# Token transforms split by symmetry, and a short convolution taken from the in-projection's banks

## The reference, cut to what matters

```python
def fourier_mix(u):                       # over tokens (L) and over 64-wide groups of channels
    g = u.reshape(B, L, FNET_GROUPS, FNET_GROUP_W)
    return jnp.fft.fftn(g, axes=(1, 3), norm="ortho").real

def hyena_mix(u, conv_w, conv_b, ..., d_bias):
    u = short_conv(u, conv_w, conv_b)     # out[t] = b + w0*u[t-1] + w1*u[t] + w2*u[t+1]
    x0, x1, v = jnp.split(u, 3, axis=-1)
    z = x1 * v
    k = hyena_filters(L, ...)             # an MLP of positions, times a decay, divided by its absolute sum
    y = irfft(rfft(z, 2L) * rfft(k, 2L))[:, :L] + d_bias * z
    return x0 * y
```

## Time and profile before

| | |
|---|---|
| median of 3 runs | 2781.29 us |
| profiled execution, its own time | 2783.26 us |
| its span | 2781.4 us |
| TensorE busy | 2525.0 us (91%) |
| VectorE, ScalarE, GpSimd busy | 1321.5, 909.1, 580.7 us |
| in-projection of layer 0 and 1 | 903.7 to 1039.3 and 1998.2 to 2100.5 us |
| `mid` of layer 0 and 1 | 1039.3 to 1147.2 and 2100.5 to 2185.9 us |

### The profile page before, as it was taken

The page is one execution under the profiler, slowest core; times in us unless marked ns, Lnnn a source line. Parts: engine busy times, 40 slices in busy tenths (PEclk is TensorE's granted clock), DMA queues, the critical chain, the costliest instruction groups (busy, mean ns, idle before and its releaser), DMA issues.

```text
span 2781.4 us, 28290 instructions
## 1 busy us (share of the span) xinstructions
PE 2525.0 (91%) x10930; PEld 1847.7 (66%) x10930; DVE 1321.5 (48%) x2006; ACT 909.1 (33%) x1468; POOL 580.7 (21%) x520
## 2 busy tenths in 40 slices
PE   6888747999997998989889999999898998999998
PEld 4664316777786884444578888888675444688886
DVE  4865545588656525443443333333534443443434
ACT  5115533322223312345433222222322355332322
POOL 1320122333331211100123122212120101222221
PEclk9997857999998999999899999999999999999999
DMA  5751101366663222200112122212132101233321
GB/s 181 235 182 31 38 0 46 114 196 197 214 209 97 71 72 86 68 18 23 38 41 79 56 62 69 69 53 64 39 114 72 57 24 37 76 91 99 99 87 57
DMA packets 71984, 240.53 MB, mean 86 GB/s; under 512 B 8303, under 2 KB 11488, under 8 KB 71852
## 3 DMA queue, kind: packets, MB, share of 16 engines
q1 hardware_dynamic: 51200, 172.64, 19.8%
q0 software_dynamic: 17600, 62.95, 7.5%
q10 hardware_dynamic: 3052, 3.13, 0.4%
HBM read 230.80 MB, written 7.90 MB: 86 GB/s over the span
## 4 chain that ended last, share of the span: by engine, by line
PE 73%; DVE 11%; ACT 5%; issue 4%; POOL 3%; DMA 3%; ACTq 0%; DVEq 0%; POOLq 0%
PE psum L461 32%; PE psum L694 19%; PE psum L1014 4%; PE psum L985 3%; DVE mod_scratch_b L1161 2%; PE psum L884 2%; DMA mod_ring_a<-in_w_mod 2%; DVE mod_scratch_a L1161 2%; PE psum L518 1%; PE psum L942 1%; PE psum L595 1%; PE psum L1000 1%; PE psum L906 1%; POOL weight_split L2432 1%; PE psum L432 1%
## 5 line engine op out<-in xcount | busy, mean ns | idle before, releaser
L461 PE MATMUL psum<-mix_split,weight_split 128*128 128x512 f32 (+1 forms) x3840 | 802.8, 370 | 25.7 <-DVE mix_split L1400 12.8
L461 PEld LDWEIGHTS psum<-mix_split,weight_split 128*128 128x128 f32 x3840 | 662.4, 190 | 167.7 <-issue 27.6
L694 PE MATMUL psum<-hidden,weight_split 128*128 128x512 f32 (+1 forms) x3072 | 633.9, 366 | 5.6 <-POOL weight_split L2432 2.9
L694 PEld LDWEIGHTS psum<-hidden,weight_split 128*128 128x128 f32 x3072 | 523.5, 188 | 112.7 <-POOL weight_split L2432 4.7
L1853 ACT CAST weight_split<-weight_ring 128x1024 fp32r<-128x1024 f32 x269 | 276.5, 1042 | 308.4 <-PE psum L694 295.7
L2432 POOL TENSOR_TENSOR weight_split<-weight_ring,weight_split 128x1024 fp32r<-128x1024 f32 x89 | 233.6, 2624 | 483.1 <-ACT weight_split L1853 482.2
L1429 DVE TENSOR_TENSOR hidden<-hidden_tmp,hidden 128x512 fp32r<-128x512 f32 (+1 forms) x128 | 136.7, 1087 | 394.0 <-POOL hidden_tmp L2581 394.0
L1077 DVE TENSOR_TENSOR weight_split<-weight_ring,weight_split 128x1024 fp32r<-128x1024 f32 x180 | 231.8, 1291 | 32.6 <-ACT weight_split L1853 32.6
L2128 ACT ACTIVATE hidden_tmp<-psum 128x512 f32<-128x512 f32 (+1 forms) x128 | 69.1, 539 | 526.4 <-PE psum L461 515.1
L461 PE MATMUL psum<-normed_in,weight_split 128*128 128x512 f32 (+1 forms) x1080 | 217.1, 362 | 9.4 <-DVE normed_in L1131 6.9
L1446 DVE SCALAR_TENSOR_TENSOR residual<-psum,modulation,residual 128x512 f32<-128x512 f32 x192 | 120.8, 658 | 213.9 <-PE psum L694 213.9
(11 more groups left out here) (277 smaller groups left out, 2420.8 us busy)
## 6 DMA issues: line engine op xcount, KB each, us to landing
weight_ring<-in_w_mlp SPq DMA_DIRECT2D x128, 512.0 KB, 3.6
mod_ring_b<-in_w_mod POOLq DMA_DIRECT2D x68, 512.0 KB, 4.0
weight_ring<-in_w_ff SPq DMA_DIRECT2D x64, 512.0 KB, 4.4
weight_ring<-in_w_in SPq DMA_DIRECT2D x45, 512.0 KB, 3.9
weight_ring<-in_tables SPq DMA_DIRECT2D x29, 512.0 KB, 3.6
mod_ring_a<-in_w_mod POOLq DMA_DIRECT2D x28, 512.0 KB, 4.6
weight_ring<-in_w_out SPq DMA_DIRECT2D x24, 512.0 KB, 3.6
weight_ring<-in_w_v SPq DMA_DIRECT2D x8, 512.0 KB, 5.3
```

The costliest lines, as they stand in the source:

```text
L461: m = pe.matmul(psum[:, b + r, 0:hi - lo], w[:, part_w, :], x[:, part_x, k, lo:hi], start=k == 0 and part_w + part_x == 0, stop=k == KT - ...
L694: mm = pe.matmul(psum[:, b + r, 0:hi - lo], w[:, part_w, :], G[:, part_x, f % (2 * GROUP), lo:hi], start=jj == 0 and part_w + part_x == 0, ...
```

## The change

- **Order of the in-projection.** A list `IN2` puts four convolution tiles first (channels of `z`'s two factors), then the rotary key, the latents, the Fourier tiles and the last two convolution tiles (the outer factor).
- **Short convolution from the banks.** Tile by tile and range by range ScalarE applies weight 1 and the bias from PSUM, VectorE adds the two shifted products from PSUM. The buffer `HU` is gone. z is made after the second and the fourth tile.
- **Norms.** Squares, sums, root, inverse and the scaling of the query latents, and all but the last broadcast for the key latents, are done beside tiles 7 to 12 of the in-projection.
- **Fourier over tokens.** `halves` makes sum and difference of a token block and the one L/2 behind it. Odd output tokens need only the difference (two rows for x), even ones only the sum; for x the sum is split once more (`FE`, made by GpSimd). Each table row is used for fewer columns.
- **Long convolution.** Tokens are taken even first, then odd (table rows, filter and decay tables, and z by a stride of 2). `multiply_spectra` computes for half the frequencies the part of the even and of the odd tokens in banks of their own, 16 matmuls instead of 32 for x; sum and difference give the frequency and its mirror. ScalarE copies the odd part, VectorE makes sums and differences (four 128x512 operations per tile), then the products for both: on each of VectorE and GpSimd three 128x512 and two 128x256 operations. These wait for both engines' products of the tile before. `back` computes even and odd tokens apart, each of half the width.
- **Smaller moves.** GpSimd issues the filter DMAs as soon as the in-projection's last matmul is done; those for c after the products of x. VectorE fills the sine input from ScalarE's copy in SBUF. The multiply by `hd` stands before the wait for the inverse. The even tokens of the output are written by strided copies.

```diff
-        out["fourier_" + name] = rows
+        odd = [np.concatenate(cos_sin(slice(i, i + P), 2, 1), 1) for i in range(0, S // 2, P)] if L == S else []
+        step = 4 if L == S else 2
+        out["fourier_" + name] = odd + [np.concatenate(cos_sin(slice(0, P), step, 0) + cos_sin(slice(0, P), step, step // 2), 1)]
+        w = w[by_parity][:, 0:L // 2]
...
+        IN2 = [(9, "conv", 2), (11, "conv", 4), (10, "conv", 3), (12, "conv", 5), (13, "rope", 0), (0, "latent", 0), (1, "latent", 1),
+               (2, "latent", 2), (3, "latent", 3), (4, "latent", 4), (5, "fourier", 0), (6, "fourier", 1), (7, "conv", 0), (8, "conv", 1)]
...
 (TensorE, in_projection_2)
+                    if i == 8:
+                        column_sums(f"qn{l}", [(SQ, 0, hi_all // P, f"qn{l}_vec", ("sum", 2))])
+                    if i == 10:
+                        b = on_all_partitions(f"qn{l}", hi_all // P)
+                    if i == 12:
+                        column_sums(f"kvn{l}", [(SQ, 0, 6, f"kvn{l}_vec", ("sum", 1))])
...
 (TensorE, over_tokens)
+                        if n < rows - 1:
+                            pe.wait_ge(*when(tag + "_vec", ("less", n)))
+                            parts = [(FA[:, 2 + n, :], L // 2, L, n == 0, n == rows - 2)]
+                        elif nm == "x":
+                            pe.wait_ge(*when(tag + "_pool", ("even", 1)))
+                            parts = [(FE[:, :], 0, P, True, True), (FA[:, 0, :], P, 2 * P, True, True)]
...
 (TensorE, multiply_spectra)
+                        bs = (take(2), take(2))
+                            for odd in range(2):
+                                for e in range(n):
+                                    m = pe.matmul(bank(bs[cs] + odd), ring_of(i, cs * L + t * P, cs * L + (t + 1) * P), IN[cs][:, t, :],
+                                                  start=e == 0, stop=e == n - 1)
...
 (VectorE, in_projection_2)
+                def conv(i, j):
+                    for r, (a, z) in enumerate(RG):
+                        ps = psum[:, bank_of[tag, i] + r, 0:z - a]
+                        ve.wait_ge(*when(tag + "_act", ("conv", j, r)))
+                        ve.scalar_tensor_tensor(out=U[:, j, a + 1:z], in0=ps[:, 0:z - a - 1], ...)
+                        ve.wait_ge(*when(tag + "_vec", ("before", j, r)))
+                        ve.scalar_tensor_tensor(out=U[:, j, a:z - 1], in0=ps[:, 1:z - a], ...)
...
 (VectorE, multiply_spectra)
+                            if (nm, f) != ("x", 0):
+                                ve.wait_ge(*when(tag + "_pool", ("y_im", *before)))
+                                ve.wait_ge(*when(tag + "_vec", ("y_re", *before)))
+                            ve.tensor_tensor(part[:, 0, :], even, odd, ALU.add)
+                            ve.tensor_tensor(part[:, 1, :], a, b, ALU.subtract)
+                        ve.tensor_tensor(w0, re[:, :, 0:HY], re[:, :, HY:512], ALU.mult)
+                        ve.tensor_tensor(w1, im[:, :, 0:HY], im[:, :, HY:512], ALU.mult)
+                        ve.tensor_tensor(w0, w0, w1, ALU.subtract)
+                        ve.tensor_tensor(Y[:, 2 * f, 0, :], w0[:, 0, :], w0[:, 1, :], ALU.add)
+                        ve.tensor_tensor(Y[:, 2 * f + 1, 0, :], w0[:, 0, :], w0[:, 1, :], ALU.subtract)
```

More of the change, by code:

```diff
@@ L796, in mid @@
                     m.then_inc(*did(tag + "_pe", ("mid", t)))
-                    freed[b] = [(tag + ("_vec" if t % 2 else "_act"), ("mid", t))]
-                column_sums(f"qn{l}", [(SQ, 0, hi_all // P, f"qn{l}_vec", ("sum", 2))])
-                def over_tokens(lo, hi, nm, works):
+                    freed[b] = [(tag + "_act", ("mid", t)) if t in (2, 3, 5) else (tag + "_vec", ("less", t))]
+                b = on_all_partitions(f"kvn{l}", 6)
+                freed[b] = freed[b + 1] = [(f"kvn{l}_vec", ("scaled", 1, 1))]
@@ L1640, in mid, with halves @@
-                short_conv(3)
-                mean(f"kvn{l}", 6, KVL)
-                inverse(f"kvn{l}", 6)
-                make_z(0)
-                diagonal(f"kvn{l}", SQ[:, 1, :], rs[:, 0:6], "inverse")
+                tag, in2 = f"mid{l}", f"in2_{l}"
+                streams = streams_of(l)
+                def halves(t):
+                    up = FA[:, t + (2 if t < 4 else 1), :]
+                    ps = bank(bank_of[tag, "mid", t])
+                    ve.wait_ge(*when(tag + "_act", ("mid", t + (2 if t < 4 else 1))))
+                    ve.wait_ge(*when(tag + "_pe", ("mid", t)))
+                    ve.tensor_tensor(FA[:, t, :], ps, up, ALU.add).then_inc(*did(tag + "_vec", ("plus", t)))
+                    ve.wait_ge(*when(tag + "_vec", ("plus", t)))
+                    ve.tensor_tensor(up, ps, up, ALU.subtract).then_inc(*did(tag + "_vec", ("less", t)))
@@ L2237, in mid @@
-                ac.wait_ge(*when(f"in2_{l}_vec", ("keep", 13, 0)))
-                ac.wait_ge(*when("gemm", (f"in2_{l}", 13)))
-                for n in range(3):
-                    square(f"qn{l}", n, LAT[:, n, :], [SQ[:, 0, :], SQ[:, 1, :], SQF], 0, hi_all)
-                for t in range(0, nq, 2):
-                    ac.wait_ge(*when(tag + "_pe", ("mid", t)))
-                    ac.copy(FA[:, t, :], bank(bank_of[tag, "mid", t])).then_inc(*did(tag + "_act", ("mid", t)))
-                root(f"qn{l}", rs[:, 0:nq])
@@ L2255, in fourier @@
+                streams = streams_of(l)
+                ac.wait_ge(*when("gemm", (in2, 13)))
+                for t in mid_tokens(l):
+                    if t in (2, 3, 5):
+                        ac.wait_ge(*when(tag + "_pe", ("mid", t)))
+                        ac.copy(FA[:, t, :], bank(bank_of[tag, "mid", t])).then_inc(*did(tag + "_act", ("mid", t)))
                 def fourier(nm, lo, hi):
+                    if nm == "x":
+                        for nm_, t in [(nm_, (h - l_) // P - 1 - d) for l_, h, nm_ in streams for d in (1, 0)]:
+                            ac.wait_ge(*filter_saved(l, nm_, t))
@@ L2256, in fourier @@
                     ac.wait_ge(*when("table", bank_of[tag, "fourier_load", nm]))
-                    ac.copy(H2[:, 4, lo:hi], psum[:, bank_of[tag, "fourier", nm], 0:hi - lo]).then_inc(*did(tag + "_act", ("fourier", nm, 0)))
-                fourier("x", 0, S)
-                short_conv(0)
-                short_conv(5)
-                if l == 0:
-                    fourier("c", S, T2)
-                short_conv(1)
+                    for step, first, a, z in fourier_parts(nm):
+                        m = ac.copy(H2[:, 4, lo + first:hi:step], psum[:, bank_of[tag, "fourier", nm], a:z])
@@ L2661, in mid @@
                 put_in(*streams[0])
+                po.wait_ge(*when(tag + "_vec", ("plus", 1)))
+                po.tensor_tensor(FE[:, :], FA[:, 0, :], FA[:, 1, :], ALU.add).then_inc(*did(tag + "_pool", ("even", 0)))
+                po.wait_ge(*when(tag + "_pool", ("even", 0)))
+                po.tensor_tensor(FA[:, 0, :], FA[:, 0, :], FA[:, 1, :], ALU.subtract).then_inc(*did(tag + "_pool", ("even", 1)))
                 multiply_spectra(*streams[0])
```

480 lines of the change are left out of this document (261 added, 219 removed).

## The result

The changed kernel takes 2707.7 us (median of 4 runs, 2700.4 to 2712.2), the kernel before beside it 2780.4 us (4 runs): a ratio of 0.974, with a 95% interval of 0.971 to 0.976. That is 73 us less where 62 were forecast, and 2708 lies in the range of 2701 to 2743. In a second comparison, of six runs, the changed kernel took 2702.7 us (0.973, 0.971 to 0.976). The profiled execution took 2712.0 us; its span fell from 2781.4 to 2710.2 us, by 71.2.

What follows compares the result with a forecast made beforehand. TensorE, busy 91%, was taken as the bound. Layer 0 gains 41.6-4.3-4.9 = 32.4 us and layer 1 37.9-3.4-4.9 = 29.6, together 62 off 2783.3, called 2720 us, range 2701 to 2743.

Steps and rivals of the forecast that it cites:

- Work removed: Fewer matmul columns in both layers' `mid` take 65.3 us of TensorE time out, at 1.68 ns a column.
- rival D: Half the columns isn't half the time, so only the forward spectra gain: 2762 us, chance 0.03.
- The front of `mid` without a wait: VectorE and GpSimd finish before TensorE asks; forward spectra start at 18.8 us in layer 0, 17.2 in layer 1.
- my three signs of being wrong: First inverse row waits too, in-projection grows over 10 us a layer, or the front of `mid` still waits for VectorE.
- Products: In `mid`, VectorE and GpSimd take turns on the spectral products, 7.2 us a round, bounds 5.3 and 8.2.
- Rival A: Products overlap at 5.3 us a round and the in-projection hides its additions: 2703 us, chance 0.2.
- Ahead of c's inverse: In layer 0's `mid` TensorE idles 7.7 us, then c's inverse takes 4.0 at low clock, ending at 66.9.
- Layer 1's second row: TensorE idles 3.8 us before layer 1's second inverse row, which then costs 3.4+1.8 us and ends at 48.5.
- The term of the moved norms: Norm sums and spread moved into the in-projection cost TensorE 4.3 us in layer 0, 3.4 in layer 1.
- the 4.9 us of added stalls and clock: In each layer's in-projection, late weight splits and low-clock restarts add 4.9 us; bounds 0, if the chain hides, and 10.
- Rivals B and C: B: products and in-projection stalls bind harder, 2740, chance 0.22. C: convolution from banks sets in-projection's pace, 2817, chance 0.02.
- my own case: The main forecast: 62 us less, 2720 us, chance 0.53.

Runs made afterwards that it cites:

- plain: Changed kernel with the Fourier, spectra and inverse transforms back at full size, with their earlier tables and product rounds: 2741.9 us, 0.986 of the kernel before.
- the version of all edits: Changed kernel with token 4's halves early, residual products before the first convolutions, all spectral products on VectorE, c's spectra before x's inverse: 2685.2 us, 0.966.
- halves: Changed kernel with layer 0's sum and difference of token block 4 (stream c) moved ahead of the norm on VectorE: 0.974 of the kernel before.
- the second profile: The changed kernel profiled once more, nothing altered, in the second comparison: 2702.7 us, 0.973 of the kernel before.
- poolprod: Changed kernel with all ten spectral products of a round on GpSimd, none on VectorE: 2731.1 us, 0.982 of the kernel before.
- dveprod: Changed kernel with all ten spectral products of a round on VectorE, none on GpSimd: 2696.3 us, 0.970 of the kernel before.

## Why the prediction was right, point by point

- **Work removed** (65.3 us at 1.68 ns a column). Busy time fell by 66.8. The plain kernel against the version of all edits, both at full clock, gives 35.4 us for layer 0 (87.1 to 51.7) and 28.9 for layer 1 (71.0 to 42.1), against 36.1 and 29.2. Half the columns is half the time: rival D is out. An inverse row of 128x256 took 3.62 as 16 records, 0.216 us apart; 128-column records cost 0.112 us from start to start (1.95 for 16 with the last one's end), near the 0.107 by columns and under the 0.137 taken.
- **The front of `mid` without a wait**: right in layer 1 (spectra at 16.2 us, forecast 17.2), wrong in layer 0 (24.5 against 18.8). The step that failed is "Each is done before TensorE asks". I counted `halves` of two blocks; the third stands behind the norm and the put-in, and I did not follow which blocks' banks `over_tokens` would take. With that bank free (halves) the spectra start at 18.0, so it cost 6.5 us here: 3.52 of wait and about 3 of low clock behind it (5.2 us in the second profile, where the low clock took 1.7). Of my three signs of being wrong this one came ("the front still waits for VectorE").
- **Products**: 7.2 us a round forecast (8 units of 0.92 us are in fact 7.4), 6.9 measured; taking turns confirmed by the two kernels that have the products on one engine. Rival A (5.3) is out. What I never asked, with all its prices on the table (0.69 and 0.42 us alone), was what VectorE alone would need: 5.05. The Trainium skill ("SBUF — State Buffer", section "SBUF: two separate sides") describes the pair of ports as "an **exclusive lock**, not a bandwidth split". The pairs above agree, 1.74 to 1.81 us against 0.61 and 1.22 alone. To the letter, with start-to-start prices, a round is 3 x 1.83 + 2 x (0.34 + 0.68) = 7.5 us; I had summed record lengths, which overlap the next by 0.04 to 0.08 us each, and so put it at 8.2. In the ten rows of the round above the ends alternate between VectorE and GpSimd, and each comes 1.12 to 1.16 us after the last (GpSimd, 128x512), 0.55 (VectorE, 128x512), 0.58 to 0.59 (GpSimd, 128x256) or 0.28 to 0.29 (VectorE, 128x256). So it is a strict taking of turns, each turn 0.06 to 0.1 us shorter than the price from start to start alone, and that makes 6.9; why it is shorter the runs don't show.
- **Two waits behind the products that I didn't list**: the values wait 1.31 us for a bank of the second round (its sums stand behind the first round's products), and x's second inverse row 1.04 us in layer 0. The profile names a copy (L1735) for the latter, but the code waits for both engines' products, and GpSimd's last ended at 1095.13, 0.15 us before.
- **Ahead of c's inverse**: 7.7 forecast, 7.38 measured, and 3.75 us for the group (4.0 forecast). It starts 67.3 us into the stage, forecast 62.9: 5.7 us late from the front, 1.3 won back behind it, 0.9 of them by the shorter rounds. c's filter landed 3.7 us after its second issue (some 4 forecast) and made TensorE wait 0.65 us. (The terms of layer 0 as I gave them add up to 41.8 us, not 41.6.)
- **Layer 1's second row**: the wait was 3.08 and not 3.8 us, and the clock stayed up: 2.2 us better. The 1.8 us that I put behind the wait are the 5.37 us of the group after a wait of 3.39 less the 3.60 of the next. No run shows that every wait of some 3 us costs them, and the earlier trace rows have one of 2.98 us with the group behind it at its full price of 3.69: I should have given that term a range.
- **The in-projection**: +3.0 us in layer 0 and +4.3 in layer 1, forecast +9.2 and +8.3. The term of the moved norms (4.3 and 3.4) is nearly all of it; the 4.9 us of added stalls and clock in each layer were mis-sized: -1.3 and +0.9 are left for them. In layer 0 the place and size of the stall were right (split ready at 936, found 936.09; 2.9 us forecast, 2.48 found), but two things fell together there: TensorE first waited for the bank that the residual operations read, which I had not named, and the split was done 0.05 us before the tile behind that wait. The second stall of 1.1 did not come, today's 0.98 and 0.83 went, and one slow tile cost 1.5, not 3.4 us. Some of it is the clock's chance: the first three tiles took 28.29 us before and 26.86 and 27.63 in the two profiles after, for the same matmuls. In layer 1 the waits are 0.67, 0.63, 1.06, 2.07 and 0.35 us, 4.8 in place of 3.9 before; the stall of 2 to 3 us at tile 3 or 4 did not come there as one wait. So the chain hid nearly all, as my lower bound said. Rivals B and C, which needed it to bind, are out.

From the first channel DFT to the attention's first score matmul layer 0 won 36.9 us (forecast 41.6) and layer 1 39.2 (37.9); with the in-projections that is 33.9 and 35.0, forecast 32.4 and 29.6. Two errors of opposite sign met in layer 0 (the front and layer 0's in-projection, 6 us each); that its sum is right to 1.5 us is luck. The remaining 2.4 of the 71.2 us lie in the rest, within its scatter.

The time itself, 2703 to 2708 us, is nearer to rival A's 2703 than to my 2720. A's half on the in-projection came: its additions were 10.2 us less than forecast in the two layers. A's half on the products did not, 6.9 us a round and not 5.3. So the range held, my own case had the mechanism of the products right, and it took too much for the in-projection.

## What to carry to other kernels

When an edit takes work off the engine that sets the pace, ask what that work was covering: here 65 us of columns brought 42 in `mid`, and 62 once the products and their order were changed (all against plain). Follow each bank to its last reader by name before you write that a front runs without a wait. And before two engines share a step, sum what the faster one needs alone: where they take turns at the memory, the helper costs its own time.

## What the runs showed of the hardware

VectorE and GpSimd on fp32 operands in SBUF take turns by the operation, not only for operations with two inputs: beside GpSimd's products two 128x256 copies from SBUF to SBUF took VectorE 2.46 us, and 0.48 in the kernel without them. VectorE's row in poolprod:

```profile
1094.35 2.46 DVE L1734 COPY spectrum_in_sin<-spectrum_in_cos 128x256 f32<-128x256 f32 x2
```

And in dveprod:

```profile
1090.10 0.48 DVE L1734 COPY spectrum_in_sin<-spectrum_in_cos 128x256 f32<-128x256 f32 x2
```

VectorE's sums in the same stretch, which take one operand from PSUM and one from SBUF, stayed at 0.68 us, but GpSimd was idle during them, so they tell nothing of that case. A copy out of PSUM beside GpSimd's products is in the trace of poolprod, and it is not held up (0.68 to 0.69 us alone):

```profile
1099.12 1.27 POOL L2727 TENSOR_TENSOR shifted<-shifted,spectrum_tmp 128x512 f32<-128x512 f32 x1
```

```profile
1099.61 0.69 DVE L1727 COPY v_heads<-psum 128x512 f32<-128x512 f32 x1 [2.80 <-PE psum L886]
```

What a wait costs in clock is not a function of its length alone. After 1.64 and 3.08 us the next group ran at the 2.4 GHz level (granted clock 1.00), after 3.52, 5.40, 7.38 and 8.06 it began at 1.2 GHz (granted clock 0.50 at the group's start). But length does not settle it: after 2.48 us in layer 0's in-projection the tile took 10.13 us and not 8.67 (granted clock 0.67 from 936.14 to 941.00), and after the same 1.06 us in layer 1's in-projection the next tile took 8.69 us in the changed kernel's profile and 10.22 in that of halves. In-projection 1 came out as 107.4 or 110.1 us for the same instructions and the same large waits.
